# Two-block transformer with 32 routed experts: expert rows scattered in four pieces to two tables, and the first four of eight final sums kept in PSUM

## The reference

```python
# T = 1024 tokens, D = 1024, 32 experts of hidden size 512, top 2 of them for each token
def expert_block(block, e):                 # rows of one expert, padded to blocks
    g, u = split(block @ w_up[e])
    return (silu(g) * u) @ w_down[e]
...
y = y[dest] * gate                          # the weight of each token's choice
f = segment_sum(y, token)                   # the two choices of a token added
x = x + mod[:, 5] * f
out = rms_norm_2(x, final_g)
```

## Time and profile before

| what | us |
|---|---|
| median of 3 runs (2862.7 to 2867.55) | 2865.32 |
| the profiled execution, whole | 2869.49 |
| its span in the trace | 2867.5 |
| of it in `experts` and the tail | about 605 |

### The profile page before, as it was taken

The page is one execution under the profiler, slowest core; times in us unless marked ns, Lnnn a source line. Parts: engine busy times, 40 slices in busy tenths (PEclk is TensorE's granted clock), DMA queues, the critical chain, the costliest instruction groups (busy, mean ns, idle before and its releaser), DMA issues. The chain is left out here.

```text
span 2867.5 us, 44001 instructions
## 1 busy us (share of the span) xinstructions
PE 2743.7 (96%) x18171; PEld 1635.5 (57%) x18171; DVE 1510.6 (53%) x2119; ACT 781.6 (27%) x1449; POOL 83.7 (3%) x138
## 2 busy tenths in 40 slices
PE   8999899999999999999999998999999799999995
PEld 4444554444444444444454445657555699999994
DVE  7886676566666667773652007867683311111114
ACT  2111771111111114511100106757332311211112
POOL 0000000000000000000000000000000011111110
PEclk9999999999999999999999998999999899999997
DMA  3022221111111117764221000004200799999996
GB/s 142 33 74 38 47 90 69 50 44 44 45 44 44 45 50 267 275 240 144 59 61 64 30 0 12 1 1 120 97 12 10 302 395 399 386 403 396 392 397 255
DMA packets 75940, 399.56 MB, mean 139 GB/s; under 512 B 13232, under 2 KB 22960, under 8 KB 59824
## 3 DMA queue, kind: packets, MB, share of 16 engines
q1 hardware_dynamic: 55440, 348.66, 33.1%
q10 hardware_dynamic: 13104, 32.52, 3.2%
q0 software_dynamic: 7280, 16.79, 1.7%
HBM read 362.66 MB, written 29.36 MB: 137 GB/s over the span
## 5 line engine op out<-in xcount | busy, mean ns | idle before, releaser
L3646 PE MATMUL ex_ps<-big,ex_xT 128*32 128x128 f32 x3072 | 348.9, 274 | 0.0
L3644 PE MATMUL ex_ps<-big,ex_xT 128*32 128x384 f32 x3072 | 344.7, 489 | 1.4 <-issue 0.7
L3646 PEld LDWEIGHTS ex_ps<-big,ex_xT 128*32 128x32 f32 x3072 | 333.7, 110 | 0.6
L1756 PE MATMUL ffn_ps<-h,V 128*128 128x512 f32 x504 | 219.7, 592 | 0.0
L2215 PE MATMUL ffn_ps<-big,V 128*128 128x512 f32 x484 | 211.3, 597 | 3.6 <-DVE V L2470 1.4
L296 DVE TENSOR_SCALAR_CACHE_REDUCE h<-ad_s_ps 128x1280 f32<-128x1280 f32 x64 | 92.9, 1489 | 177.2 <-PE ad_s_ps L205 177.2
L3644 PE MATMUL ex_ps<-ex_wd,ex_hT 128*32 128x384 f32 x1536 | 173.4, 492 | 4.3 <-DMA ex_wd<-in_w_edown 1.9
L3646 PE MATMUL ex_ps<-ex_wd,ex_hT 128*32 128x128 f32 x1536 | 175.5, 275 | 0.0
L3646 PEld LDWEIGHTS ex_ps<-ex_wd,ex_hT 128*32 128x32 f32 x1536 | 168.4, 111 | 0.6
L1756 PEld LDWEIGHTS ffn_ps<-h,V 128*128 128x128 f32 x504 | 95.8, 190 | 120.5 <-issue 120.5
L2215 PEld LDWEIGHTS ffn_ps<-big,V 128*128 128x128 f32 x484 | 92.2, 191 | 120.3 <-issue 115.0
(11 more groups left out here) (606 smaller groups left out, 4792.6 us busy)
## 6 DMA issues: line engine op xcount, KB each, us to landing
big<-in_w_eup SPq DMA_DIRECT2D x64, 2048.0 KB, 26.4
ex_wd<-in_w_edown SPq DMA_DIRECT2D x32, 2048.0 KB, 27.4
V<-in_w_down SPq DMA_DIRECT2D x35, 704.0 KB, 5.6
dn_tail<-in_w_mod ACTq DMA_DIRECT2D x48, 512.0 KB, 5.0
fm_up<-in_w_up SPq DMA_DIRECT2D x22, 1028.0 KB, 4.9
dn_tail<-in_w_in SPq DMA_DIRECT2D x17, 512.0 KB, 4.4
big<-y_dram SPq DMA_DIRECT2D x16, 512.0 KB, 7.0
f_w<-in_w_in SPq DMA_DIRECT2D x14, 512.0 KB, 4.3
```

The lines of the kernel that those rows point to most:

```text
L1756: mm = nc.tensor.matmul(bank(i, j), wj[:, k, :], bj[:, k, :], start=(k == 0), stop=(k == 3))
L3644: nc.tensor.matmul(o[32 * g:32 * g + 32, 0:W], rows(g), w[:, 0:W], start=first, stop=last)
L3646: mm = nc.tensor.matmul(o[BR:P, g * P:(g + 1) * P], rows(g), w[:, W:BANK], start=first and g == 0, stop=last and g == GR - 1)
```

## The change

`y_dram` becomes two tables of 2048 rows: `y_wide` with 768 columns and `y_rest` with 256. `move_y` and its semaphores are gone from ACT. POOL's `scatter` waits for `y_kept` instead of `moved` and issues four indirect DMAs: 96 rows of 3 KB to `y_wide`, and three times 32 rows of 1 KB to `y_rest`, straight from partitions 96 to 127. The second and third of these need the row numbers of their third in partitions 0 to 31: the router makes them with two more transposes on PE and one more DVE operation, and POOL copies them with one more small copy per block. SP loads each tile back in two DMAs (384 KB and 128 KB), 32 in all where there were 16, and both choices in the order 0, 4, 1, 5, 2, 6, 3, 7.

For tiles 0 to 3 PE now adds gate1 * f1 as well, with a second set of diagonal matrices (four DVE operations at the start of `experts`). It goes through the residual and f0 of all four tiles first and then through f1 of all four. `mix` is left for tiles 4 to 7 alone; for tiles 0 to 3 ACT squares and DVE finishes straight from PSUM. Tiles are finished and stored in the order 0, 4, 1, 5, 2, 6, 3, 7.

```diff
                 def scatter(i, u):
                     nc.gpsimd.tensor_copy(row_at[0:BR, u:u + 1], r["rows"][0:BR, bass.ds(i * 2 + u, 1)]).then_inc(row_set, 1)
-                    pool.wait_ge(row_set, i * 2 + (u + 2))
+                    nc.gpsimd.tensor_copy(third_at[0:32, u], r["thirds"][0:32, :, bass.ds(i * 2 + u, 1)]).then_inc(row_set, 1)
+                    pool.wait_ge(row_set, i * 4 + (2 * u + 3))
                     pool.sem_inc(pool_seen, 1)
-                    pool.wait_ge(moved[u], i * (16 * GR) + 16 * GR)
+                    pool.wait_ge(y_kept, i * 2 + (u + 2))
                     pool.sem_inc(pool_seen, 1)
-                    pool.indirect_dma_start(y_dram, ..., y[0:BR, u, :], None,
+                    pool.indirect_dma_start(y_wide, ..., y[0:BR, u, :], None,
                                             bounds_check=2 * T - 1, oob_is_err=False).then_inc(stored[u], 16)
+                    for g in range(GR):
+                        at = third_at[0:32, u, g - 1, :] if g else row_at[0:32, u:u + 1]
+                        pool.indirect_dma_start(y_rest, ..., y[BR:P, u, g * 2 * P:(g + 1) * 2 * P], None,
+                                                bounds_check=2 * T - 1, oob_is_err=False).then_inc(stored[u], 16)
...
-                def move_y(i, u):
-                    act.wait_ge(y_kept, i * 2 + (u + 2))
-                    for g in range(GR):
-                        act.dma_start(y[32 * g:32 * g + 32, u, 2 * W:D], y[BR:P, u, g * 2 * P:(g + 1) * 2 * P]).then_inc(moved[u], 16)
...
-                    for t in (4, 0, 5, 1, 6, 2, 7, 3) if a == 0 else range(TT):
-                        sp.dma_start(f[:, t, :], y_dram[a * T + t * P:a * T + (t + 1) * P, :]).then_inc(got[t], 16)
+                    for t in order:
+                        tile = slice(a * T + t * P, a * T + (t + 1) * P)
+                        sp.dma_start(f[:, t, 0:2 * W], y_wide[tile, :]).then_inc(got[t], 16)
+                        sp.dma_start(f[:, t, 2 * W:D], y_rest[tile, :]).then_inc(got[t], 16)
...
-                token_sum(0)
-                token_sum(1)
-                token_sum(2)
-                pe.wait_ge(y_kept, pairs * 2 + 1)
-                token_sum(3)
+                for t in range(PET):
+                    if t == PET - 1:
+                        pe.wait_ge(y_kept, pairs * 2 + 1)
+                    residual(t)
+                    weighted(t, 0, f0, got0)
+                for t in range(PET):
+                    weighted(t, 1, f1, got1)
...
-                mix(0)
-                for t in range(TT):
-                    if t + 1 < TT:
-                        mix(t + 1)
-                    finish(t)
+                for n, t in enumerate(order):
+                    if t < PET:
+                        mix(t + PET)
+                    finish(n, t)
```

More of the change, by code:

```diff
@@ L3297, in _ @@
                 nc.tensor.transpose(ids_ps[0:BR], listed[:], cst["ident"][0:NB, 0:NB]).then_inc(ids_ready, 1)
+                for g in range(1, GR):
+                    mm = nc.tensor.transpose(third_ps[0:32, g - 1, 0:NB], listed[:, 32 * g:32 * g + 32], cst["ident"][0:NB, 0:NB])
+                mm.then_inc(ids_ready, 1)
             @block.scalar
@@ L3489, in _, with experts @@
                 V_.tensor_scalar(r["rows"][0:BR, :], ids_ps[0:BR], 2.0 * T, None, ALU.add)
-def experts(nc, tag, cst, din, r, ids, h2_dram, y_dram, wu, u_ready, xb, x_ready, f0, f1, y, hid, a2, shift, h, rows, out):
+                dve.wait_ge(ids_ready, 2)
+                V_.tensor_scalar(r["thirds"][0:32], third_ps[0:32, :, 0:NB], 2.0 * T, None, ALU.add)
+def experts(nc, tag, cst, din, r, ids, h2_dram, tables, wu, u_ready, xb, x_ready, f0, f1, y, hid, a2, shift, h, rows, out):
     H = 512
@@ L3504, in experts @@
         xT = ph.sb("xT", [P, 2, KD, BR])
-        idx, row_at = ph.sb("idx", [P, 2], I32), ph.sb("row_at", [P, 2], I32)
+        idx, row_at, third_at = ph.sb("idx", [P, 2], I32), ph.sb("row_at", [P, 2], I32), ph.sb("third_at", [P, 2, 2, 1], I32)
         W = 4 * BR
+        SCATTERS = 1 + GR
+        y_wide, y_rest = tables
+        order = [t for pair in zip(range(PET), range(PET, TT)) for t in pair]
         hT = ph.sb("hT", [P, GR, P])
@@ L3692, in down, with residual @@
                     mm.then_inc(y_done, 1)
-                def token_sum(t):
+                def residual(t):
                     for k in range(KD):
@@ L3825, in weigh @@
                     V_.tensor_tensor(r["diag"], cst["ident"].unsqueeze(1).broadcast_to([P, PET, P]),
[L3826 removed]
+                                     gate[:, 0, 0:PET].unsqueeze(2).broadcast_to([P, PET, P]), ALU.mult)
+                    for t in range(PET):
+                        ins = V_.tensor_scalar(r["diag1"][t], cst["ident"], gate[:, 1, t:t + 1], None, ALU.mult)
+                    ins.then_inc(gates_ready, 1)
                 def keep_hidden(i, u):
@@ L3925, in experts_block @@
         h2_dram = nc.dram_tensor("h2_dram", (T, D), F32).ap()
-        y_dram = nc.dram_tensor("y_dram", (2 * T, D), F32).ap()
-        blk, ids, out_rows = keep("blk", [P, NB], I32), keep("ids", [P, NBI], I32), keep("out_rows", [P, NB], I32)
+        y_wide, y_rest = (nc.dram_tensor(x, (2 * T, n), F32).ap() for x, n in (("y_wide", 8 * BR), ("y_rest", D - 8 * BR)))
+        blk, ids = keep("blk", [P, NB], I32), keep("ids", [P, NBI], I32)
         count, first_expert = keep("count", [P, 3], I32), keep("first_expert", [P, 1], I32)
-        small = big[:, 20, 4 * P:4 * P + 9 * TT]
+        small = big[:, 20, 4 * P:8 * P]
         r = {"g4": small[:, 0:4 * TT].rearrange("p (t g) -> p t g", t=TT), "top": small[:, 4 * TT:5 * TT],
-             "gate": small[:, 5 * TT:7 * TT].rearrange("p (a t) -> p a t", a=2), "std": small[:, 7 * TT:8 * TT], "swapped": small[:, 8 * TT:9 * TT], "rows": out_rows[:], "block": blk[:], "count": count[:], "ids": ids[:], "first": first_expert[:],
+             "gate": small[:, 5 * TT:7 * TT].rearrange("p (a t) -> p a t", a=2), "std": small[:, 7 * TT:8 * TT], "swapped": small[:, 8 * TT:9 * TT],
+             "rows": small[:, 9 * TT:9 * TT + NB], "thirds": small[:, 9 * TT + NB:9 * TT + 3 * NB].rearrange("p (g n) -> p g n", g=2),
+             "diag1": [big[:, (18, 21)[t // 2], 8 * BR + t % 2 * P:8 * BR + (t % 2 + 1) * P] for t in range(4)], "block": blk[:], "count": count[:], "ids": ids[:], "first": first_expert[:],
              "gate5": big[:, 18, 0:8 * BR], "final": big[:, 19, :], "diag": big[:, 20, 0:4 * P].rearrange("p (t n) -> p t n", n=P)}
```

69 lines of the change are left out of this document (34 added, 35 removed).

## The result

The changed kernel takes **2930.39 us** (median of 4 runs, 2923.47 to 2934.76), the kernel before beside it 2866.44 (4 runs). The ratio is 1.022, 95% interval 1.0193 to 1.0247, so it is clearly slower, by 64 us, though not surely by more than 2%. I had forecast a gain of 11 us. The profiled execution took 2928.18 us, its span 2926.3.

The account below looks back on a forecast made before the run. PE was taken to set the pace of the expert blocks, with DMA close behind and slowing the later ones. Relief of DMA (6.3 us) plus the tail (4.3) took 2865.3 to 2854.7 us, 8-in-10 range 2850.5 to 2861.5.

Parts of the forecast that it names:

- POOL and ACT in the stage ... Both count nothing: Expert blocks: POOL's extra issues, about 5 us more per 17 us block, and ACT's three fewer cost nothing.
- Relief of DMA: Expert blocks: dropping the moves saves 0.30 us DMA work per block, so PE never waits for weights; gain 6.3 us.
- The price of such a row: Scatter in the blocks: a 1 KB packet to DRAM costs 57 ns, bounds 47 and 188 ns.
- The tail: After the last block: DVE ends at 2859.3 instead of 2863.68, gain 4.3 us.
- the prediction's last line: Signs of being wrong: turns 17.5 us apart from some block on, or PE waiting for f1.
- Rival 3: Blocks: small packets make DMA the bound earlier; 2867.4 us at 188 ns a packet; chance 0.09.
- Rival 1: Blocks: 1 KB packets cost about 120 ns, DMA's relief fails, only the tail gains; 2859.5 us; chance 0.14.
- Rival 2: Tail: POOL's last issues wait for DVE, f1 comes 3.8 us later, only the stage gains; 2857 to 2859; chance 0.15.
- The rule of the Trainium skill: Tail: by it four scatters take 8.8 us and f1 comes 0.1 us behind PE, leaving the sum unchanged.

Follow-up runs that it names:

- e3: Changed kernel without its three short scatters of 1 KB rows, so columns 768 to 1023 are not stored and output is partly wrong: 2856.46 us.
- e1: Kernel before with only the new tail; old moves, single table and one scatter kept: 2869.34 us, ratio 0.9999 to 1.0028.
- g3: Changed kernel with 64 bytes in place of 1 KB for each row of the three short scatters, output incomplete: 2929.65 us.
- h2: Changed kernel with short scatters behind the next block's gather, each issued only once the scatter ahead has landed: 3040.97 us.

## Why the prediction was wrong

- **The step that failed is "POOL and ACT in the stage ... Both count nothing".** I counted POOL's time (5 us more, of which POOL had plenty; the rows show 51.80 us busy in 200 for 26.64) and asked only who waits for POOL. Nobody does. What I left out, without a reason, was that issuing could slow an engine that waits for none of it. The cost falls on PE, which shares no semaphore with these DMAs: 2.2 us a block against the kernel before, 2.4 against e3, 64 to 74 us in all. The earlier trace rows showed two in a row, at a time when PE had no work beside them; from it I took a price for four, where the text should have given a bound above.
- **Relief of DMA, 6.3 us.** Right as a mechanism, as far as e3 shows it: blocks of 17.01 us to the end, nothing of the weights in the chain. But e3 relieves DMA by more than the change does, since it carries none of the 1 KB rows, so it does not show that 0.30 us a block would have been enough. The price of such a row, taken at 57 ns, was on the safe side: in the trace of the changed kernel (2340 to 2700 us) a packet of two rows takes 84 ns and one of a single row 47 ns, on the mean. In the changed kernel the term never came to bear, since PE was slower than DMA from the first block.
- **The tail, 4.3 us.** From the last `keep_y` 36.71 us became 32.59: 4.1. Its parts were less good. The last scatter landed 2899.58 - 2889.89 = 9.7 us after `keep_y`, not 8.2, because its last piece took 4.82 us where 3.19 were assumed. PE still went from f0 to the first f1 tile without a gap, because f0 kept it busy until then; it waited 1.8, 0.6 and 1.2 us for the next three, which was a sign of being wrong by the prediction's last line, and DVE was hardly later by it (finish 0 began 17.0 us behind `keep_y`, forecast 16.8). That the late scatter cost nothing was luck. DVE's pairs came 4.22 us apart, forecast 4.3. The trace of e1 gives 2.9 us for the tail alone; the interval of its ratio ends 0.28% above one, so no gain of its own shows in the total.
- **The rivals.** Rival 3 had the sign with the wrong mechanism: a packet's price, which g3 refutes (64 bytes for 1 KB, same time), and so do the 47 ns, far below the 168 that it needed. Rival 1 did not come. Rival 2 (POOL kept waiting by DVE in the tail) can show in one issue only, 1.28 us long instead of 0.87 beside one of DVE's additions; the next issue, beside another one, took 0.87. It is worth 0.4 us at most. None had many indirect DMAs slowing another engine.
- **The rule of the Trainium skill** in "DMA: Bandwidth & Descriptors", Rules for kernel authors (a DMA below 64 KB is mostly overhead; two disjoint halves should be one), pointed the right way. I priced it by latency and only for the tail. There the estimate by the same page's section on the anatomy of one DMA (8.9 us when added up exactly, not 8.8) came nearer than my own sum: the last piece landed 8.81 us after the first issue (2890.77 to 2899.58). It agrees in the number alone, since the four were issued 1.2 to 1.6 us apart and not one after the other's landing. My remark that two starts 1.45 us apart hide the fixed part was more than the earlier trace rows show: they have the issues, not the landings. That section's 2.0 us is below what h2 shows for one small scatter awaited, from its issue to the next: 2.9 us in quiet, 6.7 under load. None of these figures is where the loss was.

## What to carry to other kernels

Count the indirect DMAs that GpSimd issues per step, in a row. In this kernel two or three cost up to 0.4 us a block, which was as much as the change could win; four or five, 1.2 us apart, starved TensorE for some 4 us each time, whatever they carried. A wait between them was no way out while another queue filled the DMA engines. Moves between partitions that allow one scatter for four were cheap against that. Where an engine that has all its operands stalls on "issue", look at what other engines are issuing in that moment.

## What the hardware showed that I had not expected

- Four indirect DMAs in a row cut TensorE from 17 to 21 matmuls per us to about 8 and less for some 3.5 us, from 2 us after the first issue. 4 rows or 32, 64 bytes or 1 KB gave 2928.5 and 2929.7 us against 2930.4.
- In the changed kernel the DMA engines, full during the stall, fall behind it to a share of 0.31 for half a microsecond; over 200 us 351 GB/s for 396.
- A weight load or a matmul that runs within the stall takes as long as any other (109 against 110 ns, 491 against 487).
- A single scatter of 32 rows of 1 KB, awaited, takes 2.9 us at a DMA share of 0.03 and 6.7 us at a share of 0.99, from its issue to the next.
